# The byte at which TensorE's turned tokens begin inside a 256-byte line: moved from 64 to 128 for the second mixer and the feed-forward

## The chip, the cores and the metric

The kernel runs on one core of a Trainium2 chip. The metric is device time in microseconds of one execution, the median of three runs.

## The reference, cut to what matters

The reference runs two transformer blocks in sequence on 256 tokens of width 2048, all in float32. The second block is the part that the change touches:

```python
h = rms_norm_2(x, mix_norm_g)
proj = h @ w_in                       # 2048 x (3072 + 1024 + 512 + 4096)
...                                   # convolution by FFT, rope, attention give y_h and y_a
merged = g_h * (y_h @ w_br_hyena) + g_a * (y_a @ w_br_attn)
x = x + merged @ w_out                # 2048 x 2048
h2 = rms_norm_2(x, ffn_norm_g)
return x + (silu(h2 @ w_ffn_gate) * (h2 @ w_ffn_up)) @ w_ffn_down     # D_FF = 5632
```

The first block has projections of the same kind, a top-64 sparse attention and a gated recurrence, and ends in a product with `w_out` as well.

## The kernel before, in words

**Products in three parts.** Every large product `A @ W` is computed as three matmuls in the 32-bit type fp32r. Both operands are split into a high and a low part: ScalarE rounds a weight tile `raw` to `w_hi` (line 832), VectorE writes the rest `raw - w_hi` to `w_lo` (line 1365). TensorE then adds high x high, low x high and high x low in PSUM. Weights come from HBM in 1 MB loads on SyncE's queue. A chunk of 512 output columns takes eight "halves" of the split buffers.

**Turned tokens.** The contraction runs over features, so tokens have to lie with features on the partitions. TensorE transposes them (line 2342), ScalarE and VectorE copy them out of PSUM as a high and a low tile. `TURNS` and `turned_operand` (line 559) write down by hand in which slots and into which tiles: turn 0 is the first block's merged branches (`mg_hi`, `mg_lo`), turns 1 and 2 are the second mixer's input and its merged branches (both in `x1t`), turn 3 is the feed-forward's input (`hf_hi`, `hf_lo`). In turns 1 to 3 the low parts of the first two of the 16 feature rows lie apart, in `x1t_first` and `hf_first`.

**Two forms of the product.** In `by_tile` (lines 2300 to 2315) a 128x128 piece of the weights is the stationary operand and a row of turned tokens, 256 columns, is the moving one: line 2309 issues high and low tokens against `w_hi`, line 2314 high tokens against `w_lo`. A half is 24 such matmuls, 16 on line 2309 and 8 on line 2314, always in that order. The mixer's projections from the fourth chunk on, its gates and branches, and all 22 chunks of the feed-forward's gate and up products have this form. In `chunk` (line 2353 on) it is the other way round: a 128x128 piece of turned tokens is stationary and 512 columns of weights move (lines 2299, 2300, 2383); a half is 12 matmuls. So the mixer's first three chunks and the four chunks of `w_out` read `x1t`, the first block's `w_out` reads `mg_hi` and `mg_lo`, and the last product `w_ffn_down` reads `st_hi` and `st_lo` (line 3000).

**Every matmul loads new weights.** Each matmul is preceded by a load of its own stationary operand, so TensorE reads two tiles of SBUF at once: the moving operand of one matmul, and the stationary one of the next.

**Where the tiles begin.** SBUF addresses are set by hand. `LINE, PHASE, FAR = 256, 64, 128`; `spot_at(x, phase)` gives the next address after x whose remainder by 256 is `phase`. Worked out from the code, `w_hi` and `w_lo` begin at remainder 128, and so do `st_hi`, `st_lo`, `y_hi`, `y_lo`, `mg_hi` and `mg_lo`; `x1t`, `hf_hi`, `hf_lo` and the branches' `yh`, `ya_hi`, `ya_lo` begin at 64; `x1t_first` and `hf_first` begin at 128. Rows of these tiles are 1024 bytes and pieces of weights 512 bytes, so each row or piece keeps its tile's remainder. The first block's turned tokens `h_hi`, `h_lo` have rows of 1088 bytes, so their remainder steps on by 64 from row to row.

Of the kernel before, what the change touches and what calls it, by code (L numbers as in the profile page):

```python
# [16 lines left out]
F32R = mybir.dt.float32r  # L17
# [5 lines left out]
P = 128  # L23
D = 2048
T = 256
# [4 lines left out]
KT = D // P  # L30
# [33 lines left out]
def hybrid_layers(nc, a, out):  # L64

    ctx = ExitStack()
    with ctx:
        base = 4224
        spot = [base]

        def at(name, shape, dt, offset):
            return nc.alloc_sbuf_tensor_at(name, shape, dt, offset=offset)
# [47 lines left out]
        rope_at = spot[0]  # L120
# [6 lines left out]
        LINE, PHASE, FAR = 256, 64, 128  # L127

        def spot_at(x, phase):
            return x + (phase - x) % LINE  # L130

        d0 = spot[0] + (PHASE - spot[0]) % LINE
        KB = 1024
        y0 = d0 + 56 * KB
        assert y0 + 34 * KB <= nc.sbuf_usable_end, (y0 + 34 * KB, nc.sbuf_usable_end)
        f_at = h_at + (PHASE - h_at) % LINE
        hf_hi = at("hf_hi", [P, KT, T], F32R, f_at)
        hf_lo = at("hf_lo", [P, KT, T], F32R, f_at + 17 * KB)
        hf_first = at("hf_first", [P, 2, T], F32R, spot_at(d0 + 72 * KB, FAR))
        x1t_first = [at(f"x1t_first{k}", [P, T], F32R, spot_at(x, FAR)) for k, x in enumerate((f_at + 32 * KB, rope_at))]  # L140
        mg_hi = at("mg_hi", [P, KT, T], F32R, spot_at(f_at, FAR))
        mg_lo = at("mg_lo", [P, KT, T], F32R, spot_at(f_at + 16 * KB, FAR))
        assert f_at + 33 * KB <= x1_at
        y_at = spot_at(y0, FAR)
        y_hi = at("y_hi", [P, 2, BKT, T], F32R, y_at)
# [66 lines left out]


        junk2 = at("junk2", [P, D], F32, h_at)
        x1t = at("x1t", [P, 4, 2, 4, T], F32R, d0)
        filt = at("filt", [P, 2, 4, W], F32, d0 + 60 * KB)
        f_arg = at("f_arg", [P, P], F32, d0)
        f_n = at("f_n", [P, P], F32, d0 + 512)
# [341 lines left out]
        def turned_operand(e):  # L560

            def part(w):
                hi, lo = [x1t[:, w // 2, i, 2 * (w % 2):2 * (w % 2) + 2, :] if e in (1, 2)
                          else (hf_hi, hf_lo, mg_hi, mg_lo)[i + 2 * (e == 0)][:, 2 * w:2 * w + 2, :] for i in range(2)]
                rows = [lo[:, x, :] for x in range(2)]
                if w == 0 and e:
                    rows = [x1t_first[x][:, :] if e in (1, 2) else hf_first[:, x, :] for x in range(2)]
                return hi, lo, rows
            return part
# [1715 lines left out]
        def _(pe):  # L2285
# [151 lines left out]

            def merged_tile(k, i):
                cols = slice(i * P, (i + 1) * P)
                return mg_hi[:, k, cols], mg_lo[:, k, cols]  # L2440

            def warm(n, cols=W):
                for _ in range(n):
# [335 lines left out]
            for i in range(2):  # L2779
                gates(Q_P1 + 3 + i, i)  # L2780
            branches(Q_P1 + 5, 6)
            output(Q_OUT1, 0, merged_tile, 0, filter_step)


# [330 lines left out]
```

How the kernel before makes its waits and increments, by code:

```python
        @block.sync  # L589
# [6 lines left out]
            def load_unit(q, s, src, width=W, first=False):  # L596
                if not first:
                    sp.wait_ge(split_lo, 8 * q + 2 * s - 6)
                dst = raw[:, s, :, 0:width]
                if len(src.shape) == 2:
                    dst = dst.rearrange("p k n -> p (k n)")
                sp.dma_start(dst, src).then_inc(raw_in[s], 16)
# [20 lines left out]
            def load_halves(q, w, c0):  # L624
                for s in range(4):
                    sp.wait_ge(split_lo, 8 * q + 2 * s - 6)
                    sp.dma_start(raw[:, s, :, :].rearrange("p k (e n) -> p (k e) n", e=2),
                                 tile_rows(w, (s % 2) * BW, BW, slice(c0 + (s // 2) * T, c0 + (s // 2) * T + T))
                                 ).then_inc(raw_in[s], 16)
# [3 lines left out]
                    load_halves(q, w_in, c0)  # L633
                elif q:
                    load_cols(q, w_in, slice(c0, c0 + width), width)
            for j in range(3):
                load_branches(Q_P1 + j, w_branch[0], w_branch[1], slice(j * W, (j + 1) * W))
            for i in range(2):
                load_cols(Q_P1 + 3 + i, w_in, slice(C_GATES + 3 * W + i * D, C_GATES + 4 * W + i * D))
            load_branches(Q_P1 + 5, w_branch[0], w_branch[1], slice(3 * W, 4 * W))
            sp.wait_ge(sg_used, 4)
            sp.dma_start(x1[:, :, :], a["x"][0].rearrange("(b p) d -> p b d", p=P)).then_inc(x1_in, 16)
            for j in range(4):
                load_cols(Q_OUT1 + j, w_out, slice(j * W, (j + 1) * W))
```

## Time and profile before

| | |
|---|---|
| median of 3 runs | 2163.17 us (2163.07 to 2163.5) |
| the profiled execution | 2163.33 us, of which the span is 2161.5 us |
| TensorE matmuls | busy 100% of the span, 14296 instructions |
| TensorE weight loads | busy 90% |
| VectorE, ScalarE, GpSimd | 64%, 46%, 17% |
| granted TensorE clock | 1.0, the whole span |

The duration of a single matmul in the trace includes the way through the array; matmuls overlap. What one costs is the distance from its start to the start of the next, called its pitch below, and it is read from the start times of two rows and the number of matmuls between them.

### The profile page before, as it was taken

How to read it: one execution, taken by the hardware profiler on the slowest of the kernel's cores; microseconds unless marked ns; L12 is line 12 of the kernel's file. 1: busy time of each engine (PE TensorE's matmuls, PEld its weight loads, DVE VectorE, ACT ScalarE, POOL GpSimd, SP SyncE). 2: the span in 40 equal slices, each digit the busy share in tenths (PEclk: the TensorE clock that was granted, in tenths of full speed). 3: DMA queues.
4: the chain of work that ended last, by engine and by line, in shares of the span. 5: the costliest groups of instructions: out<-in, count | busy, mean ns of one | idle time of the engine just before them, and what ended most of it. 6: DMA issues, size and time to landing. Idle time of an engine off the chain costs nothing.

```text
span 2161.5 us, 34714 instructions
## 1 busy us (share of the span) xinstructions
PE 2154.4 (100%) x14296; PEld 1950.9 (90%) x14296; DVE 1374.5 (64%) x1874; ACT 1000.6 (46%) x1328; POOL 358.2 (17%) x437
## 2 busy tenths in 40 slices
PE   9999999999999999999999999999999999999999
PEld 7898889988888877899999999889999999998887
DVE  6778557968576575776786557455555555554444
ACT  6456644353354444655544445354434444444443
POOL 6563999770000000000000000000000000000000
PEclk9999999999999999999999999999999999999999
DMA  8655655545465644554456565556555555555553
GB/s 278 185 176 171 191 177 169 157 139 175 137 215 198 239 157 156 175 182 150 157 165 202 180 204 190 190 177 195 194 193 194 194 194 188 194 184 197 189 196 134
DMA packets 276530, 396.63 MB, mean 183 GB/s; under 512 B 9399, under 2 KB 198162, under 8 KB 270896
## 3 DMA queue, kind: packets, MB, share of 16 engines
q1 hardware_dynamic: 272704, 384.52, 53.9%
q0 software_dynamic: 3648, 10.37, 1.9%
q8 instruction: 81, 1.33, 0.3%
q14 instruction: 33, 0.27, 0.0%
q10 hardware_dynamic: 64, 0.14, 0.0%
HBM read 392.91 MB, written 2.10 MB: 183 GB/s over the span
## 4 chain that ended last, share of the span: by engine, by line
PE 97%; DVE 1%; ACT 0%; DMA 0%; issue 0%; SPq 0%; DVEq 0%
PE ps L2309 31%; PE ps L2314 16%; PE ps L2299 15%; PE ps L2300 14%; PE ps L2383 11%; PE ps L3000 4%; PE ps L2592 1%; PE ps L2342 0%; PE ps L2539 0%; DMA raw<-w_in 0%; PE ps L2499 0%; DVE w_lo L1365 0%; PE ps L2875 0%; PE ps L2815 0%; PE ps L2835 0%; PE ps L2748 0%
## 5 line engine op out<-in xcount | busy, mean ns | idle before, releaser
L1365 DVE TENSOR_TENSOR w_lo<-raw,w_hi 128x1024 fp32r<-128x1024 f32 x719 | 893.6, 1250 | 602.1 <-ACT w_hi L832 596.8
L832 ACT ACTIVATE w_hi<-raw 128x1024 fp32r<-128x1024 f32 x719 | 752.0, 1058 | 701.3 <-PE ps L2314 420.8
L2309 PE MATMUL ps<-hf_hi,w_hi 128*128 128x256 f32 x1408 | 329.9, 277 | 0.0
L2309 PE MATMUL ps<-hf_lo,w_hi 128*128 128x256 f32 x1232 | 288.1, 276 | 0.0
L2309 PEld LDWEIGHTS ps<-hf_hi,w_hi 128*128 128x128 f32 x1408 | 264.2, 188 | 0.1
L2299 PE MATMUL ps<-w_hi,h_hi 128*128 128x512 f32 x572 | 232.9, 407 | 0.8 <-DVE h_lo L1423 0.8
L2309 PEld LDWEIGHTS ps<-hf_lo,w_hi 128*128 128x128 f32 x1232 | 231.4, 188 | 0.0
L2309 PE MATMUL ps<-x1t,w_hi 128*128 128x256 f32 x1680 | 228.2, 280 | 0.0
L2300 PE MATMUL ps<-w_hi,h_lo 128*128 128x512 f32 x572 | 224.8, 393 | 0.0
L2309 PEld LDWEIGHTS ps<-x1t,w_hi 128*128 128x128 f32 x1680 | 209.3, 188 | 1.4 <-issue 1.0
L2314 PE MATMUL ps<-hf_hi,w_lo 128*128 128x256 f32 x1408 | 188.2, 276 | 0.0
L2314 PEld LDWEIGHTS ps<-hf_hi,w_lo 128*128 128x128 f32 x1408 | 172.7, 188 | 0.0
L2383 PE MATMUL ps<-w_lo,h_hi 128*128 128x512 f32 x572 | 155.3, 393 | 0.0
L2299 PE MATMUL ps<-w_hi,st_hi 128*128 128x512 f32 x348 | 135.5, 389 | 0.0
L2300 PE MATMUL ps<-w_hi,st_lo 128*128 128x512 f32 x348 | 135.4, 389 | 0.0
L2383 PEld LDWEIGHTS ps<-w_lo,h_hi 128*128 128x128 f32 x572 | 107.4, 188 | 24.8
L2299 PEld LDWEIGHTS ps<-w_hi,h_hi 128*128 128x128 f32 x572 | 107.5, 188 | 23.5 <-DVE h_lo L1423 1.1
L2300 PEld LDWEIGHTS ps<-w_hi,h_lo 128*128 128x128 f32 x572 | 107.8, 189 | 21.7
L2314 PE MATMUL ps<-x1t,w_lo 128*128 128x256 f32 x896 | 120.5, 277 | 0.0
L2314 PEld LDWEIGHTS ps<-x1t,w_lo 128*128 128x128 f32 x896 | 110.5, 188 | 0.0
L2309 PE MATMUL ps<-h_hi,w_hi 128*128 128x272 f32 x384 | 100.7, 295 | 0.0
L2309 PE MATMUL ps<-h_lo,w_hi 128*128 128x272 f32 x384 | 98.4, 288 | 0.0
(523 smaller groups left out, 3234.4 us busy)
## 6 DMA issues: line engine op xcount, KB each, us to landing
raw<-w_in SPq DMA_DIRECT2D x163, 1024.0 KB, 5.2
raw<-w_ffn_gate SPq DMA_DIRECT2D x44, 1024.0 KB, 5.1
raw<-w_ffn_up SPq DMA_DIRECT2D x44, 1024.0 KB, 5.1
raw<-w_ffn_down SPq DMA_DIRECT2D x44, 1024.0 KB, 4.9
raw<-w_out SPq DMA_DIRECT2D x32, 1024.0 KB, 5.1
raw<-w_branch SPq DMA_DIRECT2D x16, 1024.0 KB, 5.1
raw<-w_br_hyena SPq DMA_DIRECT2D x8, 1024.0 KB, 5.6
raw<-w_br_attn SPq DMA_DIRECT2D x8, 1024.0 KB, 5.7
```

What stands on the lines that cost most here:

```text
L832: act.activation(w_hi[:, h % 4, :, 0:width], raw[:, h // 2, 2 * (h % 2):2 * (h % 2) + 2, 0:width], ACT.Copy).then_inc(split_hi, 1)
L1365: dve.tensor_tensor(w_lo[:, h % 4, :, 0:width], raw[:, h // 2, 2 * (h % 2):2 * (h % 2) + 2, 0:width], w_hi[:, h % 4, :, 0:width].bitcast(F ...
L2299: pe.matmul(dst, left[0], w_h, start=first, stop=False)
L2300: pe.matmul(dst, left[1], w_h, start=False, stop=False)
L2309: pe.matmul(dsts[x], w_h, part, start=(k0 + e == 0 and i == 0), stop=False)
L2314: ins = pe.matmul(dsts[x], w_l, moving(k0 + e)[0], start=False, stop=(k0 + e == last))
L2383: ins = pe.matmul(dst, left(k, i)[0], w_lo[:, h % 4, e, 0:width], start=False, stop=(k == n - 1))
L2592: ins = pe.matmul(ps[6 + c][0:rows, i * (P // 2):(i + 1) * (P // 2)].rearrange("p (k n) -> p k n", n=2 ** (lev - 1)), kl[:, i, c * P:c * P ...
L3000: ins = pe.matmul(ps[bank][:, :], st_hi[:, par, s, cols], w_lo[:, h % 4, e, :], start=False, stop=last)
```

## The change

The change moves tiles in SBUF and nothing else: no instruction is added, taken away or reordered. `x1t`, `hf_hi` and `hf_lo` go from remainder 64 to 128, the remainder of the weights. The first two low rows, `x1t_first` and `hf_first`, go from 128 to 64. `hf_hi` and `hf_lo` now lie where `mg_hi` and `mg_lo` lay, and take their place in turn 0 too, at unchanged addresses. The base `d0` of the working area moves up by 256 bytes, so that all other tiles keep their remainder.

```diff
-        d0 = spot[0] + (PHASE - spot[0]) % LINE
+        x1t_at = spot_at(spot[0], FAR)
+        d0 = spot_at(x1t_at, PHASE)
...
-        hf_hi = at("hf_hi", [P, KT, T], F32R, f_at)
-        hf_lo = at("hf_lo", [P, KT, T], F32R, f_at + 17 * KB)
-        hf_first = at("hf_first", [P, 2, T], F32R, spot_at(d0 + 72 * KB, FAR))
-        x1t_first = [at(f"x1t_first{k}", [P, T], F32R, spot_at(x, FAR)) for k, x in enumerate((f_at + 32 * KB, rope_at))]
-        mg_hi = at("mg_hi", [P, KT, T], F32R, spot_at(f_at, FAR))
-        mg_lo = at("mg_lo", [P, KT, T], F32R, spot_at(f_at + 16 * KB, FAR))
+        hf_hi = at("hf_hi", [P, KT, T], F32R, spot_at(f_at, FAR))
+        hf_lo = at("hf_lo", [P, KT, T], F32R, spot_at(f_at + 16 * KB, FAR))
+        hf_first = at("hf_first", [P, 2, T], F32R, spot_at(d0 + 72 * KB, PHASE))
+        x1t_first = [at(f"x1t_first{k}", [P, T], F32R, spot_at(x, PHASE)) for k, x in enumerate((f_at + 32 * KB + 64, rope_at))]
...
-        x1t = at("x1t", [P, 4, 2, 4, T], F32R, d0)
+        x1t = at("x1t", [P, 4, 2, 4, T], F32R, x1t_at)
...
-                          else (hf_hi, hf_lo, mg_hi, mg_lo)[i + 2 * (e == 0)][:, 2 * w:2 * w + 2, :] for i in range(2)]
+                          else (hf_hi, hf_lo)[i][:, 2 * w:2 * w + 2, :] for i in range(2)]
...
-                return mg_hi[:, k, cols], mg_lo[:, k, cols]
+                return hf_hi[:, k, cols], hf_lo[:, k, cols]
```

## Rows read from the trace of the kernel before

**Rows 1.** The page: engines' busy time, and the chain by engine and line.
```profile
PE 2154.4 (100%) x14296; PEld 1950.9 (90%) x14296; DVE 1374.5 (64%) x1874; ACT 1000.6 (46%) x1328; POOL 358.2 (17%) x437
...
PE 97%; DVE 1%; ACT 0%; DMA 0%; issue 0%; SPq 0%; DVEq 0%
PE ps L2309 31%; PE ps L2314 16%; PE ps L2299 15%; PE ps L2300 14%; PE ps L2383 11%; PE ps L3000 4%; PE ps L2592 1%; PE ps L2342 0%; PE ps L2539 0%; DMA raw<-w_in 0%; PE ps L2499 0%; DVE w_lo L1365 0%; PE ps L2875 0%; PE ps L2815 0%; PE ps L2835 0%; PE ps L2748 0%
```

**Rows 2.** TensorE's groups by form: operands, xcount, busy us, mean ns.
```profile
L2314 PE MATMUL ps<-hf_hi,w_lo 128*128 128x256 f32 x1408 | 188.2, 276 | 0.0
L2314 PE MATMUL ps<-x1t,w_lo 128*128 128x256 f32 x896 | 120.5, 277 | 0.0
L2299 PE MATMUL ps<-w_hi,x1t 128*128 128x512 f32 x224 | 88.7, 396 | 0.0
...
L2309 PE MATMUL ps<-hf_first,w_hi 128*128 128x256 f32 x176 | 43.5, 280 | 0.0
...
L2309 PE MATMUL ps<-x1t_first,w_hi 128*128 128x256 f32 x112 | 27.7, 280 | 0.0
```

**Rows 3.** Timeline, TensorE, two halves of the feed-forward: start us, duration us.
```profile
1499.57 1.07 PE L2314 MATMUL ps<-hf_hi,w_lo 128*128 128x256 f32 x8
...
1502.29 1.07 PE L2314 MATMUL ps<-hf_hi,w_lo 128*128 128x256 f32 x8
...
1505.05 1.07 PE L2314 MATMUL ps<-hf_hi,w_lo 128*128 128x256 f32 x8
```

**Rows 4.** Timeline, the eight matmuls with the first two rows, feed-forward.
```profile
1503.20 0.28 PE L2309 MATMUL ps<-hf_hi,w_hi 128*128 128x256 f32 x1
1503.31 0.28 PE L2309 MATMUL ps<-hf_first,w_hi 128*128 128x256 f32 x1
...
1504.14 0.28 PE L2309 MATMUL ps<-hf_hi,w_hi 128*128 128x256 f32 x1
```

**Rows 5.** Timeline, TensorE, the mixer: first and last of the longer rows.
```profile
975.34 1.11 PE L2314 MATMUL ps<-x1t,w_lo 128*128 128x256 f32 x8
...
1087.38 1.11 PE L2314 MATMUL ps<-x1t,w_lo 128*128 128x256 f32 x8
...
1090.20 1.10 PE L2314 MATMUL ps<-x1t,w_lo 128*128 128x256 f32 x8
...
1093.03 1.10 PE L2314 MATMUL ps<-x1t,w_lo 128*128 128x256 f32 x8
...
1095.86 1.11 PE L2314 MATMUL ps<-x1t,w_lo 128*128 128x256 f32 x8
```

**Rows 6.** Timeline, TensorE, later gates of the mixer.
```profile
1227.53 1.07 PE L2314 MATMUL ps<-x1t,w_lo 128*128 128x256 f32 x8
...
1230.25 1.07 PE L2314 MATMUL ps<-x1t,w_lo 128*128 128x256 f32 x8
```

**Rows 7.** Timeline, TensorE, five halves of the mixer's w_out, tokens stationary.
```profile
1350.23 1.07 PE L2383 MATMUL ps<-w_lo,x1t 128*128 128x512 f32 x4
...
1363.96 1.07 PE L2383 MATMUL ps<-w_lo,x1t 128*128 128x512 f32 x4
```

**Rows 8.** Timeline, TensorE, four halves of w_ffn_down, tokens stationary.
```profile
1950.04 1.07 PE L3000 MATMUL ps<-w_lo,st_hi 128*128 128x512 f32 x4
...
1960.92 1.07 PE L3000 MATMUL ps<-w_lo,st_hi 128*128 128x512 f32 x4
```

**Rows 9.** Timeline, TensorE, seven halves of the first block's w_out.
```profile
767.34 1.07 PE L2383 MATMUL ps<-w_lo,mg_hi 128*128 128x512 f32 x4
...
772.20 1.07 PE L2383 MATMUL ps<-w_lo,mg_hi 128*128 128x512 f32 x4
...
788.52 1.07 PE L2383 MATMUL ps<-w_lo,mg_hi 128*128 128x512 f32 x4
```

**Rows 10.** Timeline, TensorE, a half of the first block's projections, 272 columns.
```profile
340.45 1.17 PE L2314 MATMUL ps<-h_hi,w_lo 128*128 128x272 f32 x8
...
343.48 1.17 PE L2314 MATMUL ps<-h_hi,w_lo 128*128 128x272 f32 x8
```

## The prediction, written before the changed kernel ran

> **What bounds the kernel now.** I read the page's engine line and its chain first: TensorE is busy all the span and holds 97% of the chain, VectorE and ScalarE 64% and 46% [rows 1]. Lines 2309, 2314, 2299, 2300 and 2383 make up 87% of it (31 + 16 + 15 + 14 + 11), which are the two forms of product. So TensorE's own pace is the bound, and the other engines have room for a pace that differs by a per cent. The change takes no instruction away; it can act only through the pitch of matmuls. So the next view is the timeline of TensorE, where I divide the distance between starts by the matmuls between them, and set tiles that begin at different bytes side by side.
>
> Weights begin at byte 128. With moving tokens at 64 a feed-forward half of 24 matmuls takes 1502.29 - 1499.57 = 2.72 us, a pitch of 113.3 ns [rows 3]. The half after it, whose first eight matmuls on line 2309 switch between byte 64 and the first rows at 128, takes 1505.05 - 1502.29 = 2.76 us: 0.04 us more [rows 3]; those eight have a pitch of (1504.14 - 1503.20) / 8 = 117.5 ns [rows 4]. In the mixer the same shape shows two paces with the same bytes: 2.72 us a half in the later gates [rows 6], but (1095.86 - 1087.38) / 3 = 2.827 us, a pitch of 117.8 ns, in stretches between the steps of attention and convolution [rows 5]. A slow half is known by its row of line 2314, eight matmuls in 1.10 or 1.11 us instead of 1.07; there are 19 of them, of 112 rows. Within the 456 matmuls concerned nothing waits, so a slow pace, once entered, keeps itself up until something interrupts it.
>
> With tokens stationary and weights moving, 512 columns, there is the same contrast by byte. `st` at 128: (1960.92 - 1950.04) / 4 = 2.72 us a half of 12 [rows 8]. `mg` at 128: (788.52 - 772.20) / 6 = 2.72 us [rows 9]. `x1t` at 64: (1363.96 - 1350.23) / 5 = 2.746 us [rows 7].
>
> **The change part by part.** Counts come from the groups: line 2314 issues eight matmuls a half, so 1408 / 8 = 176 feed-forward halves and 896 / 8 = 112 mixer halves; line 2299 issues four a half, so 224 / 4 = 56 halves with `x1t` stationary; the first rows are four matmuls a half, so 176 / 4 = 44 and 112 / 4 = 28 halves hold them [rows 2].
>
> *`x1t` stationary at 128.* It gets the byte at which `st` and `mg` hold 2.72 us, so I take 2.72 for 2.746: 0.026 us a half. The seven halves that hold the first rows (one a chunk, now at 64) I leave as they are. 49 x 0.026 = 1.3 us less. Bounds: 56 x 0.026 = 1.5 us less, and nothing gained.
>
> *`hf` moving at 128, weights at 128.* No row shows this steadily. What is nearest from below is the same pair of bytes with the roles exchanged: weights moving at 128 beside `st` loading at 128. There the load runs beside the first part of the matmul, and the 12 matmuls keep 2.72 us, 226.7 ns each, exactly twice the 113.3 of 256 columns [rows 3, 8]. If equal bytes made the two reads collide, that stretch would show it. So I take 113.3 ns, which changes nothing. From above there are two rows. The eight matmuls with first rows, half of which pair moving 128 with weights 128, run at 117.5 [rows 4]; and the first block's projections, whose rows step through all four remainders, take (343.48 - 340.45) / 24 = 126.3 ns, where 113.3 x 272 / 256 = 120.4 would be the same rate per column: 5.9 ns over [rows 10]. Both are reads that change their byte every few matmuls, so I think them the dearer case. They bound the price at +4.5 to +5.9 ns a matmul.
>
> *The first rows at 64.* Switching between two bytes stays, in the same 44 and 28 halves, in the opposite direction. I take the same 0.04 us a half: no change. Bounds: none left, 72 x 0.04 = 2.9 us less, and twice as much, 2.9 us more.
>
> *`x1t` moving at 128.* As for `hf`, with one thing more: the slow stretches cost 19 x (2.827 - 2.72) = 2.0 us now. The halves with stationary `mg` come back to 2.72 by themselves after an interruption (772.20 - 767.34 = 4.86 us, then 2.72 each) [rows 9], and those with `x1t` at 64 don't reach it in the stretch shown [rows 7]; that speaks for a pace at equal bytes that is found again after an interruption. I take half of the 2.0 us as gained, 1.0 us; bounds 2.0 us gained, and every mixer half slow.
>
> *What moves besides.* `mg` keeps its addresses, `d0` shifts by a whole line, no DMA, wait or order changes. I cost that at nothing; the cover is that a shift by 256 leaves every remainder, and that ScalarE and VectorE, which write the turned tiles, have half and a third of the span free [rows 1].
>
> Sum: 1.3 + 0 + 0 + 1.0 = 2.3 us less than the profiled execution's own 2163.33 us, 2161.0 us. The profiled execution lies 0.16 us above the median, within the spread of the runs, so I predict 2161.0 us for the median.
>
> The Trainium skill speaks against any effect. Its page "SBUF — State Buffer", section "Who interferes with whom", gives TensorE two read ports, one for the moving operand and one for loading weights, and calls them independent: TensorE never waits on anyone. By it the byte would not matter and the time would stay 2163.3 us. The trace agrees only in part: no engine shows up as TensorE's hindrance, but matmuls of one shape run at 113.3 and 117.8 ns with nothing waited for [rows 3, 5].
>
> **The rivals.** *Slow pace at equal bytes (slower).* The place is line 2309 and 2314 of the feed-forward, then of the mixer. If moving tokens and weights that begin at the same byte settle at the 2.827 us half, the feed-forward takes 176 x 2.827 = 497.6 us for now 132 x 2.72 + 44 x 2.76 = 480.5 us: 17.1 us more. The 93 fast mixer halves would add 93 x 0.107 - 28 x 0.04 = 8.8 us. With 1.3 us gained on the stationary tiles that is 2163.3 + 24.6 = 2187.9 us; the feed-forward alone with the other gains gives 2163.3 + 17.1 - 2.3 = 2178.1 us. It decides from 2.3 / 0.107 = 22 halves on, of 288. For it: a slow pace exists at this shape, the switching halves cost 0.04 us now, the stepping tile is dear [rows 3, 5, 10], and a switch at the head of each chunk could start it every time. Against it: the 512-column halves at equal bytes [rows 8, 9].
>
> *Slow in part.* Only some chunks fall into it, as 19 halves do now; 50 to 150 more halves give 5 to 16 us more, say 2170 us.
>
> *Everything at the fast pace.* All halves at 2.72: 1.5 us on stationary tiles, 2.0 on slow stretches, 2.9 on first rows, 2163.3 - 6.4 = 2156.9 us. For it: 2.72 is a floor that appears in every tile. Against it: the switching stays in the code.
>
> *The byte does nothing.* The 2.746 against 2.72 us would come from something else about those stages, such as the other engines' work: 2163.3 us. Against it: `mg` and `st` lie at opposite ends of the program and agree.
>
> **How the numbers follow.** Forecast 55%, between 2158 and 2164 us for itself. Slow pace throughout or in the feed-forward 24%, slow in part 8%, all fast 9%, no effect 4%. About 0.2%, 4.3 us, is what a measurement of this kernel can tell from no change, so "same" is 2158.8 to 2167.5 us. The forecast and no effect fall into it apart from a few per cent at their edges: same 0.57. All fast, and the lower edge of the forecast, give faster 0.11. The slow cases give 0.32. For eight in ten the range runs from 2157.5, short of all fast, to 2187, which takes in the feed-forward-only case and most of the full one.
>
> **What would show it.** The 12-matmul halves of line 2383 with `x1t` at 2.72 us. The feed-forward's rows of line 2314 at 1.07 us and 2.72 us apart, with 2.76 at the head of chunks. Fewer than 19 rows at 1.10 or more in the mixer. The forecast is wrong if the feed-forward's plain halves are above 2.73 us, or if `x1t` stationary stays at 2.746.

## The result, and the profile after

The changed kernel takes 2201.27 us (median of four runs, 2201.21 to 2201.79) against 2163.28 us: 1.0175 times as long, 95% interval 1.0163 to 1.0188. The forecast of 2161.0 us was wrong by 40 us, and the time lies outside the range.

The page's busy times, its row of TensorE's clock, and the chain by engine and line. Lines are one lower than in [rows 1].

```profile
PE 2192.8 (100%) x14296; PEld 1989.9 (90%) x14296; DVE 1374.7 (63%) x1874; ACT 1000.2 (45%) x1328; POOL 358.1 (16%) x437
...
PEclk9999999999999999999999999999999999999999
...
PE 97%; DVE 1%; ACT 0%; DMA 0%; issue 0%; SPq 0%; DVEq 0%
PE ps L2308 32%; PE ps L2313 16%; PE ps L2298 14%; PE ps L2299 14%; PE ps L2382 11%; PE ps L2999 4%; PE ps L2591 1%; PE ps L2341 0%; PE ps L2538 0%; DMA raw<-w_in 0%; PE ps L2498 0%; DVE w_lo L1364 0%; PE ps L2874 0%; PE ps L2814 0%; PE ps L2834 0%; PE ps L2747 0%
```

The same instructions, the full clock, no new wait, and VectorE and ScalarE as busy as before: the 38 us are all on TensorE, in lines that it already held. The page can't say more. The timeline of TensorE in the feed-forward can: start us, duration us, and the rows that answer to [rows 3, 4], with those of the mixer's gates ([rows 5, 6]), of the stationary `x1t` ([rows 7]) and of `st` ([rows 8]).

```profile
1251.29 1.12 PE L2313 MATMUL ps<-x1t,w_lo 128*128 128x256 f32 x8
...
1254.17 1.12 PE L2313 MATMUL ps<-x1t,w_lo 128*128 128x256 f32 x8
...
1371.77 1.07 PE L2382 MATMUL ps<-w_lo,x1t 128*128 128x512 f32 x4
...
1379.93 1.07 PE L2382 MATMUL ps<-w_lo,x1t 128*128 128x512 f32 x4
...
1515.49 1.12 PE L2313 MATMUL ps<-hf_hi,w_lo 128*128 128x256 f32 x8
...
1518.37 1.12 PE L2313 MATMUL ps<-hf_hi,w_lo 128*128 128x256 f32 x8
1519.33 0.28 PE L2308 MATMUL ps<-hf_hi,w_hi 128*128 128x256 f32 x1
...
1520.28 0.28 PE L2308 MATMUL ps<-hf_hi,w_hi 128*128 128x256 f32 x1
...
1521.22 1.12 PE L2313 MATMUL ps<-hf_hi,w_lo 128*128 128x256 f32 x8
...
1524.10 1.12 PE L2313 MATMUL ps<-hf_hi,w_lo 128*128 128x256 f32 x8
...
1985.24 1.07 PE L2999 MATMUL ps<-w_lo,st_hi 128*128 128x512 f32 x4
...
1996.12 1.07 PE L2999 MATMUL ps<-w_lo,st_hi 128*128 128x512 f32 x4
```

A plain half of the feed-forward is now 1518.37 - 1515.49 = 2.88 us, 120.0 ns a matmul where [rows 3] have 113.3. That is neither of the two paces known from before: 117.8 ns was the slow one [rows 5]. The half with the first rows is the *shorter* one, 2.85 us, its first eight matmuls at (1520.28 - 1519.33) / 8 = 118.8 ns. The mixer's gates take 2.88 us a half too. The stationary `x1t` is at (1379.93 - 1371.77) / 3 = 2.72 us, as forecast, and `st` stays at 2.72.

The groups by form show the same loss without any subtraction (operands, xcount, busy us, mean ns):

```profile
L2313 PE MATMUL ps<-hf_hi,w_lo 128*128 128x256 f32 x1408 | 197.6, 283 | 0.0
L2313 PE MATMUL ps<-x1t,w_lo 128*128 128x256 f32 x896 | 125.8, 283 | 0.0
```

The mean duration of one went from 276 and 277 to 283 ns [rows 2], about as much as the pitch.

To place all of it I took, for each matmul, the distance to the next start less the best pitch seen at its shape (113.33 ns for 256 columns, 226.67 for 512), left out distances of 16 ns or more above it (waits, the same within 0.2 us a group) and the last matmul before one of another shape, and added up by operand:

| us above the best pitch | before | after | all at 64 | all at 128 | weights at 192 |
|---|---|---|---|---|---|
| `hf` moving, 4224 matmuls | 1.9 | 26.9 | 17.8 | 28.1 | 3.6 |
| `x1t` moving, 2688 | 3.0 | 16.7 | 9.4 | 17.2 | 5.3 |
| `yh`, `ya` moving, 768 | 0.0 | 0.0 | 3.4 | 0.0 | 4.1 |
| `x1t` stationary, 672 | 1.6 | 0.5 | 1.6 | 0.4 | 2.0 |
| `st`, `mg` or `hf`, `y` stationary, 1823 | 0.7 | 0.7 | 0.7 | 0.7 | 4.4 |

Before to after, from the sums before rounding: 25.1 + 13.7 - 1.1 = 37.7 of the 38.0 us between the spans. The three columns on the right are experiments.

### The profile page after: what moved, and what is told of

It is laid out like the page before. It is cut to its first block, busy times and chain, and to the rows that moved or that the text cites. A ratio compares the mean times of both kernels' runs of the same rounds, so it can differ in the third digit from the quotient of the medians.

```text
span 2199.5 us, 34714 instructions
## 1 busy us (share of the span) xinstructions
PE 2192.8 (100%) x14296; PEld 1989.9 (90%) x14296; DVE 1374.7 (63%) x1874; ACT 1000.2 (45%) x1328; POOL 358.1 (16%) x437
## 4 chain that ended last, share of the span: by engine, by line
PE 97%; DVE 1%; ACT 0%; DMA 0%; issue 0%; SPq 0%; DVEq 0%
PE ps L2308 32%; PE ps L2313 16%; PE ps L2298 14%; PE ps L2299 14%; PE ps L2382 11%; PE ps L2999 4%; PE ps L2591 1%; PE ps L2341 0%; PE ps L2538 0%; DMA raw<-w_in 0%; PE ps L2498 0%; DVE w_lo L1364 0%; PE ps L2874 0%; PE ps L2814 0%; PE ps L2834 0%; PE ps L2747 0%
## 5 line engine op out<-in xcount | busy, mean ns | idle before, releaser
L2308 PE MATMUL ps<-hf_hi,w_hi 128*128 128x256 f32 x1408 | 344.7, 283 | 0.0
L2308 PE MATMUL ps<-hf_lo,w_hi 128*128 128x256 f32 x1232 | 302.7, 283 | 0.0
L2308 PEld LDWEIGHTS ps<-hf_hi,w_hi 128*128 128x128 f32 x1408 | 269.3, 191 | 0.1
L2308 PE MATMUL ps<-x1t,w_hi 128*128 128x256 f32 x1680 | 236.7, 285 | 0.0
L2308 PEld LDWEIGHTS ps<-hf_lo,w_hi 128*128 128x128 f32 x1232 | 235.8, 191 | 0.0
L2308 PEld LDWEIGHTS ps<-x1t,w_hi 128*128 128x128 f32 x1680 | 217.3, 191 | 1.4 <-issue 1.0
L2313 PE MATMUL ps<-hf_hi,w_lo 128*128 128x256 f32 x1408 | 197.6, 283 | 0.0
L2313 PEld LDWEIGHTS ps<-hf_hi,w_lo 128*128 128x128 f32 x1408 | 181.5, 192 | 0.0
L2313 PE MATMUL ps<-x1t,w_lo 128*128 128x256 f32 x896 | 125.8, 283 | 0.0
L2313 PEld LDWEIGHTS ps<-x1t,w_lo 128*128 128x128 f32 x896 | 115.5, 192 | 0.0
```

Source lines behind the costliest of these rows:

```text
L2308: pe.matmul(dsts[x], w_h, part, start=(k0 + e == 0 and i == 0), stop=False)
L2313: ins = pe.matmul(dsts[x], w_l, moving(k0 + e)[0], start=False, stop=(k0 + e == last))
```

## The experiments

The theory after this result: what counts is the distance between the byte at which the moving row begins and the byte of the weights loaded meanwhile, modulo 256. Below it is "weights minus moving": before 64, after 0. The rivals: the byte 128 of the moving row itself, or the other engines' traffic.

**Every pair of bytes by itself.** A kernel of matmuls alone; its core in outline:

```python
for wb in (0, 64, 128, 192):
    for mb in (0, 64, 128, 192):      # tiles ma..md, wa..wd begin at 0, 64, 128, 192
        spacer()                      # four matmuls of 512 columns
        # four halves of 24, four matmuls that move from mb + 64, four halves again
```

> This kernel leaves out the whole computation: it holds only matmuls of the two forms, the outputs are zeros, and no other engine works beside them. Halves of 24 matmuls of 256 columns with the moving rows at byte 0, 64, 128 or 192 and the weights at each of the four (and at 32, 96, 160, 224 beside moving 0), and halves of 12 matmuls of 512 columns with the roles exchanged. Each pair of bytes is run twice, the second time after four matmuls that move from another byte. Theory A, the relation: what counts is the distance between the byte of the moving row and the byte of the weights loaded meanwhile. Then 2.88 us a half (120.0 ns) at all four equal pairs, 2.72 us (113.3 ns) at moving 64 with weights 128 and at the other three pairs with the same distance of 64. Theory B, the byte itself: moving rows that begin at 128 are slow, 2.88 us with weights at any byte, and 2.72 us for moving 64 with any weights. Theory C, the neighbours: the pace comes from the reads and writes of ScalarE, VectorE and DMAs in the same lines; then all pairs are at 2.72 us here.

Timeline of this kernel, TensorE: `b` is byte 64, `c` is 128; the last four rows are halves of 12 with 512 columns of weights moving.

```profile
268.90 1.07 PE L83 MATMUL ps<-mb_hi,wc_lo 128*128 128x256 f32 x8
...
271.62 1.07 PE L83 MATMUL ps<-mb_hi,wc_lo 128*128 128x256 f32 x8
...
280.43 1.10 PE L83 MATMUL ps<-mb_hi,wc_lo 128*128 128x256 f32 x8
...
283.25 1.10 PE L83 MATMUL ps<-mb_hi,wc_lo 128*128 128x256 f32 x8
...
292.74 1.12 PE L83 MATMUL ps<-mc_hi,wc_lo 128*128 128x256 f32 x8
...
295.62 1.12 PE L83 MATMUL ps<-mc_hi,wc_lo 128*128 128x256 f32 x8
...
641.18 1.08 PE L95 MATMUL ps<-wc_lo,mb_hi 128*128 128x512 f32 x4
...
643.93 1.08 PE L95 MATMUL ps<-wc_lo,mb_hi 128*128 128x512 f32 x4
...
655.83 1.07 PE L95 MATMUL ps<-wc_lo,mc_hi 128*128 128x512 f32 x4
...
658.55 1.08 PE L95 MATMUL ps<-wc_lo,mc_hi 128*128 128x512 f32 x4
```

Equal bytes: 2.88 us a half. Distance 64: 2.72 us, and after the four other matmuls 2.82 us (283.25 - 280.43), with nothing else changed. All sixteen pairs, mean of the last 24 distances in ns, first and second time (one time at 512 columns, where the loaded tokens minus the moving weights is the distance):

| loaded minus moving | 256 columns, the four pairs | 512 columns, the four pairs |
|---|---|---|
| 0 | 120.0 in all eight | 226.7 in all four |
| 64 | 113.3 in four, 117.8 in four | 233.3 in all four |
| 128 | 118.5 to 120.0 | 232.1 to 233.3 |
| 192 | 117.8 in seven, 113.3 in one | 228.9 in all four |

The distances between these, run with the moving row at 0 alone, keep paces of their own at 256 columns: 118.3 ns at 32, 117.3 and 118.8 at 96, 120.0 at 160, 116.7 at 224.

Theory A holds in that the distance decides: moving 128 is slow with weights at 128 and reaches 113.3 with weights at 192, so it isn't the byte itself; and with no other engine at work the paces are the same, so it isn't the neighbours. Two things no theory had: distance 64 has two steady paces (192 as well), so that half of its eight stretches missed the 113.3 ns expected, and at 512 columns the order is another one, with equal bytes the best.

**The relation in the kernel.** The changed kernel, with the weights moved too:

```diff
+        spot[0] += 64
         w_hi = place("w_hi", [P, 4, 2, W], F32R)
         w_lo = place("w_lo", [P, 4, 2, W], F32R)
+        spot[0] += 192
```

> The changed kernel with w_hi and w_lo at byte 192 instead of 128; all moving and stationary tokens stay where the change put them. Theory A, the relation: moving 128 with weights 192 is the same distance of 64 as in the kernel before, so the feed-forward's halves return to 2.72 us and x1t's as well; with the 512-column halves of x1t back at 2.746 us too, and those of st and of turn 0 going there (87 + 32 halves by 0.026 us, 3.1 us more), 2163 to 2168 us. Theory B, the byte itself: moving 128 stays at 120.0 ns, 2201 us or more. The branches' rows, moving at 64 beside weights at 192, are a pair that no run has shown: 32 halves, at most 5 us by either.

2175.65 us (2175.37 to 2175.98). Timeline, feed-forward and `w_ffn_down`:

```profile
1501.23 1.07 PE L2315 MATMUL ps<-hf_hi,w_lo 128*128 128x256 f32 x8
...
1503.95 1.07 PE L2315 MATMUL ps<-hf_hi,w_lo 128*128 128x256 f32 x8
...
1960.40 1.07 PE L3001 MATMUL ps<-w_lo,st_hi 128*128 128x512 f32 x4
...
1963.15 1.07 PE L3001 MATMUL ps<-w_lo,st_hi 128*128 128x512 f32 x4
```

With `hf` still at 128 the plain half is back at 2.72 us: the relation, not the byte. `st`, now at distance 192, goes to 2.75 us as the map has it (12 x 228.9 ns). The total is 8 us above my range of 2163 to 2168: the branches' 32 halves, moving 64 beside weights at 192, cost 4.1 us, the stationary tokens together 4.1 instead of 3.1 us, and `hf` and `x1t` keep 4 us more than before, since some chunks stay at 117.8 ns.

**One part alone.** The changed kernel with the feed-forward's tiles put back:

```diff
-        hf_hi = at("hf_hi", [P, KT, T], F32R, spot_at(f_at, FAR))
-        hf_lo = at("hf_lo", [P, KT, T], F32R, spot_at(f_at + 16 * KB, FAR))
-        hf_first = at("hf_first", [P, 2, T], F32R, spot_at(d0 + 72 * KB, PHASE))
+        hf_hi = at("hf_hi", [P, KT, T], F32R, f_at)
+        hf_lo = at("hf_lo", [P, KT, T], F32R, f_at + 17 * KB)
+        hf_first = at("hf_first", [P, 2, T], F32R, spot_at(d0 + 72 * KB, FAR))
...
```

> The changed kernel with the feed-forward's tiles alone put back: hf at 64, hf_first at 128, turn 0 in tiles of its own again; x1t stays at 128 and its first rows at 64. If the loss is made by the matmuls that move hf and x1t themselves, and adds up, the feed-forward returns to 2.72 us a half and gives back the 26.93 - 1.86 = 25.1 us that its matmuls lost in the trace: 2176.2 us. If the pace is something of the whole program (the shift of the working area by 256 bytes, the hf tiles lying 16 instead of 17 KB apart matter for x1t too), x1t changes as well and the time is not within 2 us of that.

2176.41 us (2175.79 to 2176.51): 24.9 us given back, the parts add up, and `x1t` keeps its 16.7 us. The spacing of the `hf` tiles does nothing: they lie 16 KB apart in the run with weights at 192 too, and are fast there. Nor does the shift of the working area: it is also in the kernel with turn 2 in a tile of its own, below, where `x1t` moves 3.0 us above the best pitch as before.

**Why 512 columns misled.** Again only matmuls, always the same tiles in the same roles, with other counts of columns.

> Again only matmuls, the whole computation is left out and the outputs are zeros. Moving rows at byte 64, weights at 0, 64, 128 and 192, always the same tiles in the same roles; the matmul's columns are 128, 192, 272, 320, 384, 448 or 512. Theory A1, the timing: whether a load collides with the moving stream depends on when in the stream it runs, so on the count of columns, and not on which tile is stationary. Then with 512 columns the equal pair is at 226.7 ns and weights 64 beyond the moving row at 233.3, the reverse of 256 columns, and other counts have other best distances. Theory A2, the roles: weights loaded beside moving tokens have their best distance at 64 with any count, so 512 columns give 226.7 at distance 64 and up to 240.0 at equal bytes. Then pieces of 32, 64 and 96 stationary columns at 256 moving ones: if the loss is the load's own reads, the equal pair comes down from 120.0 towards 113.3 ns in proportion (about 115, 117, 118); if it is a fixed step it stays at 120.0. Last, distance 64 after one to four matmuls that move from another byte: both 113.3 and 117.8 are to appear, and stay to the end of the 72 matmuls.

Timeline of this kernel (24 matmuls from row to row); `mb` moves from 64, `wa`, `wb` and `wc` lie at 0, 64 and 128:

```profile
161.79 1.33 PE L85 MATMUL ps<-mb_hi,wa_lo 128*128 128x320 f32 x8
...
165.31 1.33 PE L85 MATMUL ps<-mb_hi,wa_lo 128*128 128x320 f32 x8
...
173.29 1.33 PE L85 MATMUL ps<-mb_hi,wb_lo 128*128 128x320 f32 x8
...
176.81 1.33 PE L85 MATMUL ps<-mb_hi,wb_lo 128*128 128x320 f32 x8
...
342.27 1.98 PE L85 MATMUL ps<-mb_hi,wb_lo 128*128 128x512 f32 x8
...
347.71 1.98 PE L85 MATMUL ps<-mb_hi,wb_lo 128*128 128x512 f32 x8
...
359.63 2.03 PE L85 MATMUL ps<-mb_hi,wc_lo 128*128 128x512 f32 x8
...
365.23 2.03 PE L85 MATMUL ps<-mb_hi,wc_lo 128*128 128x512 f32 x8
```

At 512 columns the equal pair takes (347.71 - 342.27) / 24 = 226.7 ns and distance 64 takes 233.3, with the weights stationary here: the count of columns makes the order, not the role. At 384 columns equal bytes and 192 are best (173.3 ns), at 448 only 192 is (200.0). At 320 columns all four distances are at 146.7 ns. At 272 columns distance 64 is at 123.3, equal bytes at 125.2, the two others at 126.7. At 128 and 192 columns every distance settles at 111.7 ns, the same for both counts, so the moving columns don't set the pace there; that the loads do is likely, but no run separates it.

With fewer stationary columns the loss does not shrink in proportion, the order changes: equal bytes 113.3 ns with 32 columns, 120.0 with 64, 115.9 with 96. So the orders that A1 forecast hold and my proportional estimate does not; that the reason is the time at which a load runs is not shown.

Of the twelve starts at distance 64 after one to four matmuls from another byte, five went on at 113.3 and seven at 117.8 ns, each to its end. The byte makes no rule, but the number nearly does: one and four matmuls gave 117.8 in all six starts, three gave 113.3 in all three, two gave 113.3 twice and 117.8 once. The starts with one and two came out of 117.8 ns and those with three and four out of 113.3, so number and pace before are not told apart. Four matmuls changed the pace every time, here in three starts and in the map in four.

**The first rows at the byte of the rest.** The kernel before with all rows of `hf` and `x1t` at 64 (the start of the edit is shown), and the changed kernel with all at 128 (the opposite edit):

```diff
-        hf_first = at("hf_first", [P, 2, T], F32R, spot_at(d0 + 72 * KB, FAR))
+        hf_first = at("hf_first", [P, 2, T], F32R, spot_at(d0 + 72 * KB, PHASE))
...
```

> The kernel before with the first low rows of the second mixer and the feed-forward at byte 64 like the rest, so that no row of a half switches bytes. Theory A with two steady paces at distance 64: the rows at the other byte are what a half pays 0.04 us for, and also what may push it from one pace into the other. If the chunks start at 113.3 ns by themselves, the 44 feed-forward and 28 mixer halves give back 72 x 0.04 = 2.9 us: 2160.4 us. If they start at 117.8 ns and nothing pushes them back, the feed-forward loses 17 us and the mixer up to 9: up to 2189 us. Half of the starts each way, as in the map, would be about 2174 us. Under the theory that the byte alone counts, all rows at 64 are fast: 2160.4 us or less.

2189.58 us, 1.0120 times before (1.0104 to 1.0135). Timeline, the mixer's branches, and the start and end of the feed-forward's halves (line 2985 forms the row scales, between two halves):

```profile
1341.06 1.10 PE L2314 MATMUL ps<-yh,w_lo 128*128 128x256 f32 x8
...
1343.88 1.10 PE L2314 MATMUL ps<-yh,w_lo 128*128 128x256 f32 x8
...
1468.54 1.07 PE L2314 MATMUL ps<-hf_hi,w_lo 128*128 128x256 f32 x8
...
1471.26 1.07 PE L2314 MATMUL ps<-hf_hi,w_lo 128*128 128x256 f32 x8
1472.17 0.59 PE L2985 MATMUL ps<-dg,onesq 128*128 128x256 f32 x2
...
1474.48 1.11 PE L2314 MATMUL ps<-hf_hi,w_lo 128*128 128x256 f32 x8
...
1915.44 1.11 PE L2314 MATMUL ps<-hf_hi,w_lo 128*128 128x256 f32 x8
...
1918.27 1.11 PE L2314 MATMUL ps<-hf_hi,w_lo 128*128 128x256 f32 x8
```

The feed-forward starts at 2.72 us, is interrupted by line 2985 at 1472.17, and is at 2.83 us from then to its end, 446 us later. `yh` and `ya`, whose bytes nobody moved, run at 2.82 us here: they got the pace from the halves ahead of them. The kernel before has `yh` at 2.72 us, and it has the same interruption, with another end:

```profile
1331.13 1.07 PE L2314 MATMUL ps<-yh,w_lo 128*128 128x256 f32 x8
...
1333.85 1.07 PE L2314 MATMUL ps<-yh,w_lo 128*128 128x256 f32 x8
...
1461.74 0.59 PE L2985 MATMUL ps<-dg,onesq 128*128 128x256 f32 x2
...
1464.05 1.11 PE L2314 MATMUL ps<-hf_hi,w_lo 128*128 128x256 f32 x8
...
1466.85 1.07 PE L2314 MATMUL ps<-hf_hi,w_lo 128*128 128x256 f32 x8
```

Behind line 2985 the row of line 2314 is slow (1.11 us) there too. Between it and the next lie the first rows at byte 128, and the next is fast. The row of line 2314 behind line 2985 is slow in each of the seven kernels here that hold `hf` 64 bytes from the weights. So the rows at another byte, which I had costed as a price of 0.04 us a half, are what brings the fast pace back; they come twice a chunk, and without them the kernel loses 26 us.

> The changed kernel with the first low rows at 128 too: every moving row at the byte of the weights. Theory A: the halves that held the rows at 64 go from 2.854 to 2.880 us, 72 x 0.026 = 1.9 us more, 2203.2 us. If it is the switching that costs, as the prediction had it, 72 halves get 0.04 us cheaper: 2198.4 us.

2202.57 us (2202.5 to 2202.85), 1.3 us more than the change: plain halves and halves with first rows alike at 2.880 us. At equal bytes there is one pace and nothing to push.

**Moving rows at 64 with stationary tokens at 128, and other bytes for the first rows.** From the kernel before, turn 2 alone gets its own tile at 128:

```diff
+        x1t_out = at("x1t_out", [P, 4, 2, 4, T], F32R, x1t2_at)      # x1t2_at = d0 - 192, byte 128
...
-                hi, lo = [x1t[:, w // 2, i, 2 * (w % 2):2 * (w % 2) + 2, :] if e in (1, 2)
+                hi, lo = [(x1t, x1t_out)[e - 1][:, w // 2, i, 2 * (w % 2):2 * (w % 2) + 2, :] if e in (1, 2)
...
```

> The kernel before with a tile of its own at byte 128 for turn 2 alone, the stationary tokens of the mixer's w_out; what moves as rows stays at 64. By the trace of the changed kernel the 512-column halves with x1t then take 2.72 instead of 2.746 us: 32 x 0.026 = 0.8 us less, 2162.5 us. If the loss at 512 columns is not a matter of the relation of the two bytes, 2163.3 us.

2162.78 us (2162.53 to 2163.3) against 2163.31: 0.9997, interval 0.9988 to 1.0006, no difference that this measurement can tell. In the trace it is there: `x1t` stationary falls from 1.6 to 0.9 us above the best pitch, its halves at (1377.98 - 1361.66) / 6 = 2.72 us.

```profile
1361.66 1.07 PE L2390 MATMUL ps<-w_lo,x1t_out 128*128 128x512 f32 x4
...
1377.98 1.07 PE L2390 MATMUL ps<-w_lo,x1t_out 128*128 128x512 f32 x4
```

On top of it, `hf_first` and `x1t_first` at 192 or at 0 in place of 128:

> The kernel with turn 2 in a tile of its own (2162.8 us measured), and the first low rows of the second mixer and the feed-forward at byte 192 instead of 128; the other rows stay at 64, the weights at 128. The kernel with all rows at 64 took 2189.6 us, so some rows at another byte are what keeps the fast pace. If any other byte does that, 2162.8 us within 3 us (the price of the 72 halves with the rows may change from 0.04 us to 0.02 or 0.06). If only first rows at the weights' own byte do it, the feed-forward runs at 117.8 ns again: about 2188 us.

> The same with the first low rows at byte 0. If any other byte does it, 2162.8 us within 3 us; if only the weights' own byte does, about 2188 us.

2179.17 us at 192 (1.0072, 1.0058 to 1.0086) and 2164.54 us at 0 (1.0005, 0.9996 to 1.0014). At 192 the mixer stays fast (2.9 us above the best pitch) and the feed-forward is 18.1 us above it, as with all rows at 64; at 0 it is 2.3 us above. With the rows at 192 the half behind line 2985 is slow, and the next one stays so, though the first rows lie between:

```profile
1463.96 1.11 PE L2316 MATMUL ps<-hf_hi,w_lo 128*128 128x256 f32 x8
...
1466.79 1.11 PE L2316 MATMUL ps<-hf_hi,w_lo 128*128 128x256 f32 x8
```

So neither "any other byte" nor "only the weights' byte": two of the three other bytes push the feed-forward back to the fast pace. Why 192 doesn't stays open. Rows at 192 lie at distance 192 from the weights, the one that has the pace of 117.8 ns in the map as well; whether that is the reason, no run shows.

## Why the prediction was wrong

**The step that failed** is "`hf` moving at 128, weights at 128": I took 113.3 ns at no cost, from `st` and the weights at equal bytes with 512 columns [rows 8]. The pair costs 120.0 ns: 6.67 ns x 4224 = 28.2 us, less 1.1 for the 44 halves that are 0.026 us shorter and 1.9 that those halves cost before, 25.2 us (25.1 in the table). The analogy fell because which distance is good depends on the count of columns; 512 columns are best just where 256 are worst. The load "runs beside the first part of the matmul" with 512 columns only. The loads of the kernel before, by form:

```profile
L2314 PEld LDWEIGHTS ps<-hf_hi,w_lo 128*128 128x128 f32 x1408 | 172.7, 188 | 0.0
...
L3000 PEld LDWEIGHTS ps<-w_lo,st_hi 128*128 128x128 f32 x348 | 65.3, 188 | 13.6
```

A load takes 188 ns in the trace at both shapes. That is less than the 226.7 ns between two matmuls of 512 columns, and more than the 113.3 of 256, where each load therefore runs on beside the matmul after. So the one could not stand for the other; that this makes the order of the distances, no run shows.

**The bounds were dismissed, and even they were short.** I had +4.5 to +5.9 ns from the eight first-row matmuls and from the 272-column tile [rows 4, 10], and called them the dearer case because they change their byte. The map shows 117.8 and 120.0 with no change of byte at all, and 272 columns at 123.3 to 126.7 with constant bytes. The dear rows were near the ordinary price; the cheap ones [rows 3] were the special case. The rival "slow pace at equal bytes" had place and sign right. It took 117.8 ns and gave 2187.9 us; at 120.0 ns its sum is 132 x 2.880 + 44 x 2.854 = 505.7 us for 480.5 in the feed-forward, and with the mixer's 13.7 more and 1.1 less on the stationary tiles 2201.1 us.

**`x1t` moving at 128** failed the same way: 13.7 us lost instead of 1.0 gained. **The first rows at 64**: forecast 0.04 us a half dearer than plain halves, as before; in the feed-forward they are 0.026 us *cheaper*, below even the bound of no price. And reading the 0.04 us of before as a cost of switching missed what the switch buys.

**`x1t` stationary at 128** was right: 1.3 us less forecast, 1.1 measured. **What moves besides** was right: nothing.

The rule of the Trainium skill in "SBUF — State Buffer", section "Who interferes with whom", by which TensorE's two reads are independent and it never waits, would have given 2163.3 us. The map disagrees: with every other engine idle the pitch of one shape goes from 113.3 to 120.0 ns by the two bytes alone.

## What to carry to other kernels

Where each matmul loads new weights, the byte of the moving row and the byte of the load are one setting, to be read at the very shape that is used: a row from another count of columns may have the opposite order. When a trace shows a shape at two paces with the same operands, the fast one can't be counted on; ask what brings it back, and take care of an odd row that looks like a cost. A kernel of bare matmuls that steps through the pairs settles in 730 us what a trace of the whole can only suggest.

## What the runs showed that I had not expected

- One 128x128x256 fp32r matmul with a new load each has several steady pitches by two bytes alone: in the kernel 113.3, 117.8 and 120.0 ns, that is 272, 283 and 288 cycles at the full 2.4 GHz, in the map some between them too. The pace at distance 64 is a state that outlives the tile: from `x1t` to `yh` and `ya`, and over 446 us of the feed-forward.
- With 128 and 192 columns the pitch settles at 111.7 ns at each of four distances; with 320 columns at 146.7.
- The mean load of `w_lo` beside `hf` rows takes 192 ns after and 188 before, though its size is the same. That the two reads collide is the likely reading of all this; no run here shows it, nor in which unit.
